# Recurrent mixer's level scores in tiles of 32 rows, and a new order of the steps in the mixers and at the seams

## The chip, the cores and the metric

The kernel runs on one core of a Trainium2 chip. The time is the device time of one execution in microseconds (us). TensorE is called PE, VectorE DVE, ScalarE ACT, GpSimd POOL and the engine that issues loads SP.

## The reference

x has 256 rows of 1024. It goes through two blocks of two layers each, all in float32. Every layer is a mixer and a gated feed-forward part (2816 wide), each added to x, with norms between:

```python
first_block:  x = x + retention_nsa_mixer(rmsnorm(x))      # stage 0
              x = x + swiglu(rmsnorm(x))                   # stage 1
              x = x + hgrn2_mixer(rmsnorm(x))              # stage 2
              x = x + swiglu(rmsnorm(x))                   # stage 3
              x = rmsnorm(x)
second_block: x = layer_norm(ALPHA * x + diff_attention(x))   # stage 4
              x = layer_norm(ALPHA * x + swiglu_2(x))         # stage 5
              x = layer_norm(ALPHA * x + chunk_attention(x))  # stage 6
              x = layer_norm(ALPHA * x + swiglu_2(x))         # stage 7
```

The recurrent mixer (stage 2) has 8 heads of 128 and computes, chunk by chunk,

```python
decay = jnp.exp(jnp.where(causal, b[:, :, :, None, :] - b[:, :, None, :, :], -jnp.inf))
attn = jnp.sum(qc[:, :, :, None, :] * decay * kc[:, :, None, :, :], axis=-1)
o = einsum(attn, vc) + einsum(qc * jnp.exp(b), state)
```

where b is the running sum of the logarithms of the forget gates. Since the decay stands inside the sum over the channels, the kernel splits the pairs (row, earlier row) by levels of 64, 32, 16, 8, 4, 2 and 1 rows: within one level the decay is a product of a factor of the row and a factor of the earlier row, and the scores of a level are matrix products.

## The kernel before

**Products.** All weights are streamed in pieces of 128x1024 numbers ("chunks", numbered through the whole program, 403 of them). SP loads a chunk into one of 4 buffers `raw`. ACT rounds it to `whi` (L2053, step HI) and POOL writes the rest `wlo = raw - whi` (L2353, step LO), each into one of 6 buffers. PE multiplies the high and low parts of the activations (`xx`, `mh`/`ml`, `hh`/`hl`) with `whi` and the high part with `wlo` (L1079, L1080, L1086). A unit is the work on one chunk for one half of the rows: four instructions with `whi` and two with `wlo`, for 128 rows and 512 columns. There are 662 units; HI of chunk c waits for the unit that used chunk c-6 last, the load of chunk c waits for LO of chunk c-4. The middle of the feed-forward stages multiplies with the weights as the stationary side (L1105, L1108).

**Side steps.** Everything else is cut into steps with two letters and a key: for instance XT (L1134) turns a quarter of x with four transposes, XH (L2099, L2102) and XL (L1471, L1475) split it into high and low parts on ACT and DVE; RES, BN, AG, RS and AP are residual, statistics and norm; SC and DC are score products (L1212, L1217) of the attentions, MK the maximum, EX the exponentials (L2201), RC and CB2 (L1659 to L1675) the combination of the two softmaxes in stage 4, TR turns the weights (L1253), AV multiplies with v. P1, P2 and P3 (L1986 to L1999, L2325) compute the scalar lambda of stage 4, RO (L1759 to L1767) is the rotation, KT turns q and k. In the recurrent mixer H1 (L1353, L1356) sums the logarithms, H2 takes exponentials on ACT, H3 (L1934 to L1938) multiplies heads and decays on DVE, H4 (`level_scores`, L1366 to L1378) is the level scores on PE, H5 (L1946, L1948) and HA collect them and O1 (L1395 to L1402) multiplies with v. A key of the mixer is (head, t), t the half of 128 rows.

**Order.** `PLAN` is a table of text, one for each of the 8 stages: "18: RC 0 0; CB2 0 0; DC 0 1 @2; TR 0 0" says that these steps stand behind unit 18 of the stage; @2 names the PSUM tile. A minus marks a step that belongs to the stage before. Every engine walks through the same table and picks its own steps, so it determines the order of instructions on each engine, between the units on PE and between the splits HI on ACT and LO on POOL. Waits are semaphores that each step counts up.

PE's tile: a product whose stationary side has 64 or 32 columns, or whose sum runs over 64 or 32 rows, uses a part of PE's array (128x64, 128x32, 64x128, 32x32); several such parts can work on different instructions. A float32 product is run in two passes, and shows as two records in the trace.

Of the kernel before, what the change touches and what calls it, by code (L numbers as in the profile page):

```python
# [17 lines left out]
FF = 2816  # L18
# [117 lines left out]
NQ, N5, N6, RQ, RK, RV, RG = 0, 512, 1024, 1304, 1816, 2328, 2840  # L136
# [172 lines left out]
62: MH 3
63: ML 3  # L310
65: RES 0 0; SQ 0 0; XT 0 0; RES 1 0
66: XH 0 0; XT 1 0; XL 0 0; XH 1 0
# [4 lines left out]
1: -SQ 0 1; -SQ 1 1; -XT 0 1; -XT 1 1; -XH 0 1  # L317
2: -RS 1; -XL 0 1
# [48 lines left out]
70: RES 0 0; SQ 0 0; B3; XT 0 0  # L367
71: XH 0 0
72: XL 0 0
74: RES 0 1; SQ 0 1; XT 0 1  # L370
# [8 lines left out]
0: -RES 1 1; -XT 1 1  # L379
1: -XH 1 1  # L380
# [2039 lines left out]
```

How the kernel before makes its waits and increments, by code:

```python
            def load(c):  # L945
                name, at, n = STREAM[c]
                if c >= NR:
                    e.wait_ge(s_lo, c - NR + 1)
                e.dma_start(raw[c % NR][:, 0:n], a[name][at:at + 128 * n].rearrange("(p m) -> p m", p=128)
                            ).then_inc(d_raw[c % NR], 16)
# [6 lines left out]
            def feed(c):  # L957
# [9 lines left out]
                    e.dma_start(w1c[:, 0, :], a["cw1k"]).then_inc(d_cw, 16)  # L967
                if c == 9:
                    e.dma_start(w2c[:, 0:64], a["cw2k"]).then_inc(d_cw, 16)
                    e.dma_start(w2c[:, 64:128], a["cw2k"]).then_inc(d_cw, 16)
                    e.dma_start(w2c[:, 128:192], a["cw2v"]).then_inc(d_cw, 16)
                if c == 10:
                    e.dma_start(w1c[:, 1, :], a["cw1v"]).then_inc(d_cw, 16)
                if c == 14:
                    e.dma_start(LC[:, 0:1024], a["ret"]).then_inc(d_ret, 16)
                if c == first[1] + 12:
                    e.wait_ge(S["R4"], 2)
                    e.dma_start(LC[:, 0:1152], a["hg"][:, 0:1152]).then_inc(d_hg, 16)
                if c == first[1] + 14:
                    e.wait_ge(s_unit, BEGIN[1])
# [2 lines left out]
                    e.dma_start(HM[:, :], a["hg"][:, 1152:1344]).then_inc(d_hn, 16)  # L983
                if c == first[3] + 12:
                    e.wait_ge(S["H5"], 16)
                    e.dma_start(GB[:, 0, :], a["fng"].partition_broadcast(128)).then_inc(d_fn, 16)
# [458 lines left out]
            def own():  # L1445
                e.wait_ge(s_dve, dv.n)
```

## Time and profile before

| | |
|---|---|
| median of three runs | 1295.08 us (1291.74 to 1297.9) |
| the profiled execution | 1292.82 us, span 1291.0 us |
| PE busy | 1275.3 us (99%) |
| POOL busy | 1030.8 us (80%) |
| ACT busy | 773.4 us (60%) |
| DVE busy | 486.0 us (38%) |
| granted TensorE clock | 0.998 |
| read from HBM | 222.59 MB, 173 GB/s |

The profile is one execution. Its timeline gives for each row the start and the length in us, the engine, the line, the operation, the tiles written and read, and in brackets how long the engine sat idle before it and what ended that. Matmuls overlap each other, so the distance between two starts says what one costs, not its length. The stages begin at these times: 0 at 0, 1 at 151, 2 at 337, 3 at 497, 4 at 684, 5 at 800, 6 at 987 and 7 at 1099 us.

### The profile page before, as it was taken

The numbers are of one execution on the slowest core, as the hardware profiler recorded it, in microseconds if no ns is written. First come the engines' busy times: TensorE is split into PE (matmuls) and PEld (weight loads), VectorE is DVE, ScalarE is ACT, GpSimd is POOL, SyncE is SP. The second block draws the span as 40 slices with busy tenths as digits, with TensorE's granted clock in tenths as the row PEclk, the third lists the DMA queues.
The fourth block names the chain that finished last, engine by engine and source line by source line (L and its number), as shares of the span: only waits on it lengthen the run. The fifth ranks groups of instructions, "written<-read, shape, count | busy, mean of one in ns | idle before, by whom it ended". The sixth has DMA issues, their size and how long they took to land.

```text
span 1291.0 us, 20471 instructions
## 1 busy us (share of the span) xinstructions
PE 1275.3 (99%) x7642; PEld 1065.2 (83%) x7642; DVE 486.0 (38%) x1080; ACT 773.4 (60%) x1481; POOL 1030.8 (80%) x874
## 2 busy tenths in 40 slices
PE   9999999999999999999999999999999999999997
PEld 7877888888888878888887787888887888888886
DVE  3465423331166752333105556232203254333302
ACT  6656576654688776666445675565534565556631
POOL 6666798878977548888889678888889987988874
PEclk9999999999999999999999999999999999999999
DMA  8443476655544425666556445666665644576552
GB/s 280 157 130 115 132 238 202 188 169 190 180 148 146 131 71 180 203 186 193 176 191 184 149 143 155 217 198 207 186 190 170 226 148 147 184 227 193 184 176 82
DMA packets 63122, 224.97 MB, mean 174 GB/s; under 512 B 7344, under 2 KB 7984, under 8 KB 63024
## 3 DMA queue, kind: packets, MB, share of 16 engines
q1 hardware_dynamic: 62736, 223.57, 55.1%
q8 instruction: 61, 1.00, 0.3%
q14 instruction: 37, 0.30, 0.1%
q10 hardware_dynamic: 288, 0.10, 0.0%
HBM read 222.59 MB, written 1.05 MB: 173 GB/s over the span
## 4 chain that ended last, share of the span: by engine, by line
PE 94%; POOL 2%; ACT 1%; DMA 1%; DVE 1%; issue 0%; SPq 0%; ACTq 0%; DVEq 0%
PE G L1079 17%; PE G L1086 17%; PE G L1080 17%; PE G L1105 10%; PE A L1105 10%; PE A L1108 5%; PE G L1108 5%; POOL wlo L2353 2%; PE A L1217 1%; PE A L1253 1%; PE A L1134 1%; DMA raw<-in_w_a 1%; PE A L1277 1%; PE A L1395 0%; PE A L1356 0%; PE A L1375 0%
## 5 line engine op out<-in xcount | busy, mean ns | idle before, releaser
L2353 POOL TENSOR_TENSOR wlo<-raw,whi 128x256 fp32r<-128x256 f32 (+2 forms) x866 | 1021.3, 1213 | 242.5 <-ACT whi L2053 242.0
L2053 ACT ACTIVATE whi<-raw 128x1024 fp32r<-128x1024 f32 x403 | 422.9, 1057 | 188.3 <-PE G L1086 162.9
L1079 PE MATMUL G<-whi,xx 128*128 128x512 f32 (+1 forms) x560 | 224.4, 401 | 3.5 <-DVE xx L1475 2.4
L1080 PE MATMUL G<-whi,xx 128*128 128x512 f32 (+1 forms) x560 | 216.8, 388 | 0.0
L1086 PE MATMUL G<-wlo,xx 128*128 128x512 f32 (+1 forms) x560 | 171.3, 388 | 0.2 <-POOL wlo L2353 0.2
L1105 PE MATMUL A<-xx,whi 128*128 128x512 f32 x576 | 144.6, 393 | 0.0
L1105 PE MATMUL G<-xx,whi 128*128 128x512 f32 x576 | 144.2, 392 | 0.0
L1079 PE MATMUL G<-whi,hh 128*128 128x512 f32 x352 | 137.4, 390 | 0.0
L1080 PE MATMUL G<-whi,hl 128*128 128x512 f32 x352 | 137.0, 389 | 0.0
L1079 PEld LDWEIGHTS G<-whi,xx 128*128 128x128 f32 x560 | 105.3, 188 | 27.8 <-issue 5.7
L1086 PEld LDWEIGHTS G<-wlo,xx 128*128 128x128 f32 x560 | 104.4, 188 | 23.0 <-POOL wlo L2353 0.6
L1080 PEld LDWEIGHTS G<-whi,xx 128*128 128x128 f32 x560 | 105.4, 188 | 18.5
L1105 PEld LDWEIGHTS A<-xx,whi 128*128 128x128 f32 x576 | 103.7, 189 | 18.7
L1105 PEld LDWEIGHTS G<-xx,whi 128*128 128x128 f32 x576 | 103.6, 189 | 18.5
L1086 PE MATMUL G<-wlo,hh 128*128 128x512 f32 x352 | 108.4, 389 | 0.0
L1108 PEld LDWEIGHTS A<-xx,wlo 128*128 128x128 f32 x576 | 78.6, 190 | 5.6
L1108 PEld LDWEIGHTS G<-xx,wlo 128*128 128x128 f32 x576 | 78.6, 190 | 5.6
L1108 PE MATMUL G<-xx,wlo 128*128 128x256 f32 x576 | 80.3, 282 | 0.0
L1108 PE MATMUL A<-xx,wlo 128*128 128x256 f32 x576 | 80.3, 282 | 0.0
L1086 PEld LDWEIGHTS G<-wlo,hh 128*128 128x128 f32 x352 | 66.1, 188 | 13.8
L1079 PEld LDWEIGHTS G<-whi,hh 128*128 128x128 f32 x352 | 66.1, 188 | 13.5
L1080 PEld LDWEIGHTS G<-whi,hl 128*128 128x128 f32 x352 | 66.1, 188 | 13.5
(385 smaller groups left out, 1504.4 us busy)
## 6 DMA issues: line engine op xcount, KB each, us to landing
raw<-in_g SPq DMA_DIRECT2D x88, 512.0 KB, 4.0
raw<-in_u SPq DMA_DIRECT2D x88, 512.0 KB, 4.2
raw<-in_d SPq DMA_DIRECT2D x88, 512.0 KB, 4.0
raw<-in_w_h SPq DMA_DIRECT2D x32, 512.0 KB, 3.6
raw<-in_w_e SPq DMA_DIRECT2D x24, 512.0 KB, 3.7
raw<-in_w_a SPq DMA_DIRECT2D x24, 512.0 KB, 3.7
raw<-in_w_b SPq DMA_DIRECT2D x24, 512.0 KB, 3.5
raw<-in_w_eo SPq DMA_DIRECT2D x8, 512.0 KB, 3.5
```

Source lines behind the costliest of these rows:

```text
L1079: e.matmul(o, sh[:, kt, xs], whi[h][:, ws], start=u.first and j == 0, stop=False)
L1080: e.matmul(o, sl[:, kt, xs], whi[h][:, ws], start=False, stop=False)
L1086: m = e.matmul(o, sh[:, kt, xs], wlo[h][:, ws], start=False, stop=u.stop and final)
L1105: e.matmul(o[:, :], whi[h][:, 128 * kt:128 * kt + 128], xx[:, kt, :], start=kt == 0, stop=False)
L1108: m = e.matmul(o[:, 0:256], wlo[h][:, 128 * kt:128 * kt + 128], xx[:, kt, 0:256], start=False, stop=kt == u.kts[-1])
L1134: m = e.transpose(A[t][:, 512 * b + 128 * i:512 * b + 128 * i + 128], X[:, t, 512 * b + 128 * i:512 * b + 128 * i + 128], ident)
L1217: m = e.matmul(tile[:, at:at + nk], qs[i], ks[i], start=not mask, stop=True, skip_group_check=True)
L1253: m = e.transpose(tile[0:kp, (i * nb + b) * 128:(i * nb + b) * 128 + 128], s[:, 2 * i if key[0] == 4 else i, 128 * b:128 * b + kp], ident)
L1277: m = e.matmul(heads4(tile[64 * g:64 * g + 64, 0:256], 2), v, wt[:, g:4:2, b, :], start=b == 0, stop=b == nb - 1, skip_group_check=True)
L2053: e.activation(whi[c % NH][:, 0:n], raw[c % NR][:, 0:n], ACT.Copy).then_inc(s_hi, 1)
L2353: m = e.tensor_tensor(wlo[c % NH][:, i:j], raw[c % NR][:, i:j], whi[c % NH][:, i:j].bitcast(F), ALU.subtract)
```

## The change

It has two parts. The first is in `level_scores`. The product of 64 rows becomes two of 32 rows, and for t = 1 the product of 128 rows becomes four of 32:

```diff
-                e.matmul(tile[0:64, 64:128], M[:, 128:192], M[:, 192:256], start=False, stop=False, skip_group_check=True)
+                for j in range(2):
+                    e.matmul(tile[32 * j:32 * j + 32, 64:128], M[:, 128 + 32 * j:160 + 32 * j], M[:, 192:256],
+                             start=False, stop=False, skip_group_check=True)
...
                 if t == 1:
-                    m = e.matmul(tile[:, 128:256], HX[:, 128 * (h % 4):128 * (h % 4) + 128], M[:, 0:128],
-                                 start=True, stop=True, skip_group_check=True)
+                    for j in range(4):
+                        c = 128 * (h % 4) + 32 * j
+                        m = e.matmul(tile[32 * j:32 * j + 32, 128:256], HX[:, c:c + 32], M[:, 0:128],
+                                     start=True, stop=True, skip_group_check=True)
```

The two diagonal products of 32x32 and the 24 small ones behind them stay as they are. That makes 40 instructions more on PE (6829 before, 6869 now).

The second part is the table `PLAN`. No step is added or removed and no unit moves; about 300 entries change their place, nearly all in stages 0, 2, 4 and 6 and at the seams. The order of POOL and SP is the same. Some lines of it (first a line of stage -1/0, then of stages 2, 4, 4, 5):

```diff
--1: -XT 0 0; -SQ 0 0; -XH 0 0; HI 0; -XL 0 0; -XT 0 1; LO 0; -XH 0 1
+-1: -XT 0 0; -SQ 0 0; -XH 0 0; -XL 0 0; HI 0; -XT 0 1; LO 0; -XT 1 0; -XH 0 1
...
-29: FJ 1; H4 0 1; H3 1 0; H1 1 1 @1
-30: H5 0 1; HA 0 1; H4 1 0; H2 1 1; GB 0 @2; HA 1 0; GC 0; EV 3 1
-31: H5 1 0; H3 1 1; T1 1 @0
-32: GF 0; H4 1 1; FB 2 @2
+28: H1 1 0 @0; H3 0 1; H2 1 1; H3 1 0; H1 1 1 @1; H4 0 1
+30: HA 0 1; H5 0 1; H4 1 0; HA 1 0; H3 1 1; GC 0; GB 0 @2; EV 3 1; H4 1 1
+31: H5 1 0; T1 1 @0
+32: GF 0; FB 2 @2
...
-2: -AP 1 1; -XT 0 1; P1; -XT 1 1; -XH 0 1
-3: P2; -XL 0 1; -XH 1 1; P3
-4: -XL 1 1; MB
-5: RO 0 0
+2: -XL 1 0; -AP 0 1; -AP 1 1; -XT 0 1; -XH 0 1
+3: -XT 1 1; -XL 0 1; -XH 1 1
+4: -XL 1 1; RO 0 0; P1; P3; MB
+6: P2
...
-18: RC 0 0; CB2 0 0; DC 0 1 @2; TR 0 0
-19: MK 0 1; EX 0 1
+18: RC 0 0; DC 0 1 @2; CB2 0 0
+19: TR 0 0; MK 0 1; EX 0 1
...
-93: AG 0; RS 0
-94: AP 0 0
-95: AP 1 0; XT 0 0; XH 0 0; XT 1 0; XL 0 0; RES 1 1
+92: RES 1 0; BN 1 0; AG 0; RS 0
+94: AP 0 0; XT 0 0; XH 0 0
+95: AP 1 0; XT 1 0; XL 0 0; RES 1 1
```

At the seam of stages 4 and 5 the entry XH 0 0 stands on ACT ahead of the split of the second feed-forward chunk instead of behind it.

The order of instructions, engine by engine, at three of these places. Line numbers of the changed kernel are lower, since its table is shorter. First PE in stage 4, before: the second tile of scores (L1212, L1217 on `G`), the turn of the first tile's weights (L1253), then a product unit.

```order
L1086 MATMUL G<-wlo,xx 128x512 x2
L1212 MATMUL G<-MB,IB 128x2x128 x2
L1217 MATMUL G<-KTa,QTa 128x256 x4
L1253 MATMUL A<-CN,W 128x128 x2
L1079 MATMUL G<-whi,xx 128x512
L1080 MATMUL G<-whi,xx 128x512
```

And in the changed kernel:

```order
L1070 MATMUL G<-wlo,xx 128x512 x2
L1196 MATMUL G<-MB,IB 128x2x128 x2
L1201 MATMUL G<-KTa,QTa 128x256 x4
L1063 MATMUL G<-whi,xx 128x512
L1064 MATMUL G<-whi,xx 128x512
L1063 MATMUL G<-whi,xx 128x512
L1064 MATMUL G<-whi,xx 128x512
L1070 MATMUL G<-wlo,xx 128x512 x2
L1237 MATMUL A<-CN,W 128x128 x2
```

The turn of the weights now stands one unit later.

Second DVE at the beginning of stage 4, before: the lambda steps (`AG`, `SM<-SM`) stand between the low parts of x (`xx<-A,xx`) and ahead of the rotation (`RT`, `PJ<-G,RT`).

```order
L1495 SCALAR_TENSOR_TENSOR X<-X,SM,LC 128x512 x2
L1986 TENSOR_TENSOR AG<-AG 128x64 x2
L1989 TENSOR_SCALAR AG<-AG 128x128
L1992 TENSOR_REDUCE SM<-AG 128x1 x2
L1475 TENSOR_TENSOR xx<-A,xx 128x4x128
L1997 TENSOR_TENSOR SM<-SM 128x1
L1999 TENSOR_SCALAR SM<-SM 128x1
L1475 TENSOR_TENSOR xx<-A,xx 128x4x128
L1624 CAST IB<-CN 128x128
L1625 CAST MB<-CN 128x128
L1759 SCALAR_TENSOR_TENSOR RT<-G,CN 128x8x32
```

And in the changed kernel:

```order
L1483 SCALAR_TENSOR_TENSOR X<-X,SM,LC 128x512 x2
L1463 TENSOR_TENSOR xx<-A,xx 128x4x128 x2
L1747 SCALAR_TENSOR_TENSOR RT<-G,CN 128x8x32
L1749 SCALAR_TENSOR_TENSOR RT<-G,CN 128x8x32
L1752 SCALAR_TENSOR_TENSOR G<-G,CN 128x512
L1755 TENSOR_TENSOR PJ<-G,RT 128x512
L1974 TENSOR_TENSOR AG<-AG 128x64 x2
L1977 TENSOR_SCALAR AG<-AG 128x128
L1980 TENSOR_REDUCE SM<-AG 128x1 x2
L1985 TENSOR_TENSOR SM<-SM 128x1
```

Both low parts of x and the first rotation now stand ahead of the lambda steps.

Third PE at the seam of stages 5 and 6, before: the last unit of stage 5 (`hh`, `hl`), two turns of a quarter of x in one row, the first unit of stage 6.

```order
L1086 MATMUL G<-wlo,hh 128x512 x2
L1134 MATMUL A<-CN,X 128x128 x8
L1079 MATMUL G<-whi,xx 128x512
L1080 MATMUL G<-whi,xx 128x512
L1079 MATMUL G<-whi,xx 128x512
```

And in the changed kernel:

```order
L1118 MATMUL A<-CN,X 128x128 x4
L1063 MATMUL G<-whi,hh 128x512
L1064 MATMUL G<-whi,hl 128x512
L1063 MATMUL G<-whi,hh 128x512
L1064 MATMUL G<-whi,hl 128x512
L1070 MATMUL G<-wlo,hh 128x512 x2
L1118 MATMUL A<-CN,X 128x128 x4
L1063 MATMUL G<-whi,xx 128x512
```

One of the two turns now stands ahead of the last unit.

## Rows read from the trace of the kernel before

**Rows 1.** The page, part 4: the chain that ended last, by engine.
```profile
PE 94%; POOL 2%; ACT 1%; DMA 1%; DVE 1%; issue 0%; SPq 0%; ACTq 0%; DVEq 0%
```

**Rows 2.** Who PE waited for: total us, times, longest.
```profile
PE G L1079 <- DVE xx L1475: 2.4, 3, 1.1
PE A L1253 <- DVE W L1675: 2.2, 1, 2.2
```

**Rows 3.** Timeline of PE, small steps in stages 2 and 4.
```profile
375.67 0.62 PE L1086 MATMUL G<-wlo,xx 128*128 128x512 f32 x2
376.22 0.33 PE L1366 MATMUL A<-W 128*64 128x64 f32 x2
376.48 0.22 PE L1368 MATMUL A<-W 128*32 128x32 f32 x2
...
376.55 0.52 PE L1375 MATMUL A<-W 128*32 128x32 f32 x36
...
377.10 0.50 PE L1079 MATMUL G<-whi,xx 128*128 128x512 f32 x1
...
382.99 0.49 PE L1378 MATMUL G<-W,HX 128*128 128x128 f32 x2
383.23 0.36 PE L1353 MATMUL A<-Wr,lf 128*128 128x256 f32 x1
...
417.23 0.42 PE L1402 MATMUL A<-PJ,DG 32*32 32x128 f32 x8
...
767.37 0.62 PE L1086 MATMUL G<-wlo,xx 128*128 128x512 f32 x2
767.82 0.60 PE L1253 MATMUL A<-CN,W 128*128 128x128 f32 x4
```

**Rows 4.** Timeline of DVE, one step of decays and the instruction behind it.
```profile
378.53 0.28 DVE L1934 TENSOR_TENSOR W<-G,QK 128x128 f32<-128x128 f32 x1
...
380.09 1.39 DVE L1886 TENSOR_TENSOR lf<-A,lf 64x512 fp32r<-64x512 f32 x2
```

**Rows 5.** Timeline of POOL at the start.
```profile
12.92 18.69 POOL L2353 TENSOR_TENSOR wlo<-raw,whi 128x1024 fp32r<-128x1024 f32 x13 [0.25 <-ACT whi L2053]
```

**Rows 6.** Timeline of all engines, beginning of stage 4.
```profile
688.35 1.03 DVE L1986 TENSOR_TENSOR AG<-AG 128x64 f32<-128x64 f32 x2 [0.34 <-DMA AG<-in_alam]
688.47 0.60 ACT L2102 ACTIVATE xx<-A 128x512 fp32r<-128x512 f32 x1 [1.50 <-PE A L1134]
...
690.26 0.68 DVE L1475 TENSOR_TENSOR xx<-A,xx 128x512 fp32r<-128x512 f32 x1
...
690.99 0.50 PE L1079 MATMUL G<-whi,xx 128*128 128x512 f32 x1 [0.74 <-DVE xx L1475]
```

**Rows 7.** Timeline of POOL, ACT and PE, first weights of stage 4.
```profile
693.82 19.54 POOL L2353 TENSOR_TENSOR wlo<-raw,whi 128x256 fp32r<-128x256 f32 x28 [0.35 <-ACT whi L2053]
...
712.52 1.06 ACT L2053 ACTIVATE whi<-raw 128x1024 fp32r<-128x1024 f32 x1 [4.27 <-DMA raw<-in_w_a]
...
717.21 0.44 PE L1253 MATMUL A<-CN,W 128*128 128x128 f32 x2 [2.20 <-DVE W L1675]
...
717.40 0.47 PE L1079 MATMUL G<-whi,xx 128*128 128x512 f32 x1
```

**Rows 8.** Timeline of PE and ACT, seam of stages 4 and 5.
```profile
797.53 0.60 PE L1134 MATMUL A<-CN,X 128*128 128x128 f32 x4
797.72 1.06 ACT L2053 ACTIVATE whi<-raw 128x1024 fp32r<-128x1024 f32 x1 [0.29 <-PE G L1086]
...
798.69 0.58 ACT L2102 ACTIVATE xx<-A 128x512 fp32r<-128x512 f32 x1
```

**Rows 9.** Timeline of DVE and PE, seam of stages 5 and 6.
```profile
982.80 0.75 DVE L1504 SCALAR_TENSOR_TENSOR X<-G,SM,LC 128x512 f32<-128x512 f32 x1 [0.33 <-ACT SM L2038]
...
985.17 1.04 PE L1134 MATMUL A<-CN,X 128*128 128x128 f32 x8
...
987.28 0.47 PE L1079 MATMUL G<-whi,xx 128*128 128x512 f32 x1 [1.07 <-DVE xx L1475]
```

More of the change, by code:

```diff
@@ L302 @@
-53: WL 2 1 1; R5 0; EV 6 1; GS 1; R1 1 @1
-54: R2V 1; R2A 1; GT 1; R6 0; R3 1; R7 0
+16: TT 0 @2
+18: TT 1 @1; CA 0 @2; CA 1 @0; CE 0; CB 0; TC 2; TT 2 @1; CD 0; EV 2 0; CB 1; CD 1; CG 0; MK 1 0 0
+19: CF 0
+20: SC 1 0 0 @1; MK 0 0 1; CE 1
+21: EX 1 0 0; EV 2 1; GE; TC 3; CF 1; EX 0 0 1; CG 1; SC 0 0 1 @2
+22: GD; NW 1 0 0
+23: TT 3 @0; NW 0 0 1; MK 1 0 1
+24: SC 1 0 1 @0
+25: RO 0 0; TR 1 0 0; CPA 1 0 0; EX 1 0 1; CPA 0 0 1
+27: AV 1 0 0; TR 0 0 1; NO 1 0 0
+28: NW 1 0 1; SC 0 0 0 @1; MK 0 0 0; AV 0 0 1; NO 0 0 1
@@ new lines @@
+43: NW 0 1 0; NW 1 1 1; WL 2 0 0; TR 0 1 0; TR 1 1 1; SC 0 1 1 @2; CPA 0 1 0; MK 0 1 1; AV 0 1 0
+44: CPA 1 1 1; NO 0 1 0; EX 0 1 1; CPV 1 1 1; SC 2 1 0 @0; AV 1 1 1; EV 5 0
+45: EX 2 1 0; NO 1 1 1; MK 2 1 0; SC 2 1 1 @1; CPA 2 1 0; EV 5 1; EX 2 1 1; WH 2 1 0
+46: NW 0 1 1; NW 2 1 0; TR 2 1 0
+47: MK 2 1 1; AV 2 1 0; NA 2 1 0; TR 0 1 1
+49: WL 2 1 0; NW 2 1 1; R1 0 @0
+50: CPA 0 1 1; GS 0; TR 2 1 1; EV 6 0; GT 0; R2V 0; CPV 2 1 1; R2A 0; CPA 2 1 1
+51: NO 0 1 1; R3 0; AV 0 1 1; AV 2 1 1
+52: NA 2 1 1; WH 2 1 1
@@ L304 @@
+53: R4 0; WL 2 1 1; EV 6 1; GS 1; R1 1 @1
+54: R5 0; R2V 1; R2A 1; R6 0; R3 1; GT 1; R7 0
 55: R4 1; R8 0
-57: R5 1; MT 2 @0; R6 1
-58: MH 2; ML 2; R7 1
-59: R8 1
+57: R5 1; MH 2; MT 2 @0; R6 1; R7 1
+59: R8 1; ML 2
 61: MT 3 @0
[L309 to L312, printed above, removed]
+62: ML 3; MH 3
+65: RES 0 0; XT 0 0; RES 1 0; SQ 0 0
+66: XH 0 0; XT 1 0; XH 1 0; XL 0 0
 68: XL 1 0
@@ L366 @@
 69: B2
[L367 to L370, printed above, removed]
+70: RES 0 0; SQ 0 0; XT 0 0; B3
+72: XH 0 0
+74: RES 0 1; XL 0 0; SQ 0 1; XT 0 1
 75: XH 0 1
 76: XL 0 1
-92: RES 1 0; SQ 1 0; XT 1 0
-93: XH 1 0
+92: RES 1 0; XT 1 0
+93: SQ 1 0; XH 1 0
 94: XL 1 0; RS 0
@@ L403 @@
-35: H2 2 0; FD 2
-36: FE 2
+18: FB 1 @1; FJ 0
+19: FA 1; EV 2 0
+20: H1 0 0 @0; T1 0 @2; FD 1; TV 0
+21: FE 1
+22: TA 0; H2 0 0; EV 2 1
+23: FG 1; H2 0 1; HA 0 0; EV 3 0
+24: H2 1 0
+25: H1 0 1 @2; FF 1; H3 0 0
+26: H4 0 0
+27: FJ 1; H5 0 0
+28: H1 1 0 @0; H3 0 1; H2 1 1; H3 1 0; H1 1 1 @1; H4 0 1
+30: HA 0 1; H5 0 1; H4 1 0; HA 1 0; H3 1 1; GC 0; GB 0 @2; EV 3 1; H4 1 1
+31: H5 1 0; T1 1 @0
+32: GF 0; FB 2 @2
+33: H5 1 1; FA 2; HA 1 1; TV 1
+35: FD 2
+36: FE 2; EV 4 0
 37: FF 2
-38: EV 4 0
-39: FG 2; EV 4 1; TA 1; GC 1; EV 5 0; H2 2 1; HA 2 0; H2 3 0
@@ new lines @@
+46: H5 2 1; H4 3 0; H2 3 1; O1 0 @0; H5 3 0; HA 3 0; H3 3 1; T1 2 @2; H4 3 1; H5 3 1
+47: O2 0; HA 3 1; O3 0; TA 2; TV 2; EV 5 1; MH 0; H2 4 0
+48: H1 4 0 @1; MT 0 @0
+49: ML 0; H3 4 0
+50: H1 4 1 @0; FB 3 @2; H2 4 1; H4 4 0
+51: H5 4 0; FA 3; HA 4 0; H3 4 1
+52: H4 4 1; H1 5 0 @1; EV 6 0; FD 3; HA 4 1; H2 5 0; FE 3
+53: H5 4 1; H3 5 0; H1 5 1 @0
+54: H4 5 0; HA 5 0; H2 5 1; FG 3; EV 6 1; FF 3; H5 5 0
+55: H3 5 1
+56: O1 1 @1; O2 1; T1 3 @2; FJ 3; HA 5 1; H4 5 1; H5 5 1; O3 1
+58: H1 6 0 @0; TA 3; TV 3; MT 1 @1
@@ L539 @@
 51: RC 3 1; CB2 3 1
[L540 to L543 removed]
+52: TR 3 1; CPA 3 1; MH 2
+53: AV 3 1; ML 2; MT 2 @0; NQ 3 1
+55: NF 3 1; MT 3 @1
 56: MH 3
@@ L704 @@
 74: RES 0 1; BN 0 1
-92: RES 1 0; BN 1 0
-93: AG 0; RS 0
-94: AP 0 0
-95: AP 1 0; RES 1 1; BN 1 1; AG 1; RS 1; AP 0 1; AP 1 1
+81: RES 1 0
+85: BN 1 0
+89: AG 0
+92: AP 0 0; AP 1 0; RES 1 1
+93: RS 0
+95: BN 1 1; AG 1; RS 1; AP 0 1; AP 1 1
 """,
```

274 lines of the change are left out of this document (108 added, 166 removed).

## The prediction

> **What bounds the kernel now.** I read the page first. PE carries 94% of the chain that ended last [rows 1], and by the table above it is busy for 1275.3 of 1291.0 us. So only two things can shorten the program: fewer or cheaper instructions on PE, or fewer of its waits. Next the table of PE's own waits [rows 2]: three waits for DVE's last step at a seam (`xx`, L1475) are 2.4 us together, one wait in stage 4 (`W`, L1675) is 2.2 us. Then the timeline of single stretches, for what one step costs and what ended each wait [rows 3 to 9].
>
> A difference of 0.5% (6.5 us) is about what a measurement of this kernel can tell from no change.
>
> The sum is made against the profiled execution, 1292.82 us (span 1291.0). The median of the three runs is 1295.08 us, 2.3 us above it; the change of the sum is applied to that median.
>
> **Level scores in 32 rows.** One step of level scores (L1366 to L1375) lasts from 376.22 to 377.10, 0.88 us, when a product follows [rows 3]. Its first instruction, 64 rows wide, goes as two passes and holds PE for 0.26 us, until the narrow ones start at 376.48. The change cuts it into two of 32 rows in different column groups, so that the whole step has one shape of tile. What two narrow pieces with 64 columns cost no row shows. Bounds: nearly nothing, if other narrow pieces cover them (0.03 us); or four passes in a row. From 376.55 on, 36 narrow passes of 32 columns take 0.52 us in four column groups, some 0.03 us a pass within one group if four run side by side, so 0.06 us for 64 columns and 0.23 us for four in a row. I take two passes in each of two groups side by side, 0.12 us, since the eight passes of 32x32 with 128 columns last 0.42 us together [rows 3], which they could not one after another at the 0.12 us of a pass of L1378 (below). That is 0.14 us less per step, 16 steps: **-2.2 us** (bounds -3.7 and -0.5).
>
> For t=1 the square product L1378 goes from 128 rows to four pieces of 32. It starts at 382.99 and the next step at 383.23, 0.24 us for two passes. Four groups side by side need the same two passes of 128 columns, 0.22 us, and PE stays in one shape of tile. I take 0.02 us less, 8 steps: **-0.2 us**. If the pieces ran in a row, eight passes of 0.11 us, it would be +0.64 us a step; that is a rival below.
>
> **Changes of the tile's shape.** From the last pair of product instructions to square transposes PE needs 0.45 us (767.37 to 767.82), to a 64-row piece 0.55 us (375.67 to 376.22) [rows 3]. So a change of the tile's shape costs some 0.09 us. Counted over PE's instructions in their order, the kernel before has 165 such changes and the changed one 138. Of the 27 fewer, 16 lie inside the level scores and are in the term above. The other 11 come from small steps now standing next to others of their shape: **-1.0 us**. The Trainium skill, TensorEngine Tiling (Array Packing), Key Properties, says that changing the tiling mode drains the engine; the 0.09 us agree with it.
>
> **The start.** PE now turns the third quarter of x before its first product. ACT can then split it sooner, and POOL, which sat idle 0.25 us at 12.92 and then ran 13 pieces without a break [rows 5], starts that chain 0.25 us earlier. PE waits for this chain once, in block 1. **-0.25 us**.
>
> **Stage 4, first wait.** On DVE the products for lambda (from 688.35) stand ahead of the step that PE's next product needs, which starts at 690.26 although ACT had written its input by then; PE waits 0.74 us until 690.99 [rows 6]. The new order puts the lambda steps behind that step and behind the first rotation. With ACT done at 689.07 the step ends before PE asks at 690.25. What is late next is nothing on PE; lambda itself is wanted only at the first combination, 25 us later. That is 0.9 us that PE gains here, 0.16 of it the engine's own restart. Moved along is one tiny exponential on ACT, behind two splits of later weights.
>
> **Stage 4, second wait.** PE has issued the second tile of scores and then waits 2.20 us for the first tile's weights, until 717.21 [rows 7]. In the new order one product unit (six instructions of 0.227 us, 1.36 us) stands between. The weights hang on ACT: it splits a piece that landed late (712.52, 4.27 us idle for the DMA) ahead of the exponentials. That load was issued when POOL had finished seven pieces in a row from 693.82 on, with 0.35 us idle ahead of them. So the weights come at most 0.35 us sooner, 716.86, however early PE is. Before, the second product unit after the scores starts at 717.40 + 1.36 = 718.76. Now it starts at 716.86 + 0.19 (the two transposes) = 717.05. Both waits together: **-1.7 us**, not the 3.3 us that the two seem worth, and PE still waits 1.3 us there.
>
> **Seam of stages 4 and 5.** The turned x is ready at 797.53 + 0.60 = 798.13, but ACT starts the split of a weight at 797.72 and reaches it at 798.69; PE then waits for the last of the three waits of [rows 2], 2.4 - 0.74 - 1.07 = 0.6 us [rows 8]. In the new order the split stands behind. That is 0.56 us sooner: **-0.55 us**. The weight split is used some twelve units later.
>
> **Seam of stages 5 and 6.** DVE has normed the first quarter at 982.80 + 0.75 = 983.55, yet PE turns it at 985.17, behind the last product unit, and waits 1.07 us until 987.28 [rows 9]. Now the turn stands one unit earlier, so ACT and DVE work under that unit. The wait goes, 1.2 us with the restart. Late next is the third quarter: DVE norms it only behind the residual and the statistics of the last one, and with PE 1.2 us ahead I expect 0.2 us before its turn and 0.2 us before the product after. **-0.8 us** (bounds -1.2 and 0).
>
> **Waits that the new order adds.** About thirty other PE steps are moved by one to three units, and in the trace most have 0.2 to 1.4 us between their last input and their start, which is less than a unit. Their inputs on DVE and ACT are moved too. No row shows what is left over. Bounds: 0, and 4 us (a quarter of a unit at a dozen places). I take **+0.6 us**, nearer to nothing, since where I followed the order by hand (the first heads of the recurrent mixer, the second pair of stage 6) the inputs came in time.
>
> Sum: -2.2 -0.2 -1.0 -0.25 -1.7 -0.55 -0.8 +0.6 = **-6.1 us**. That gives 1286.7 us for the profiled execution and **1289.0 us** for the median, 0.47% less: at the edge, but within 0.5%.
>
> **Rivals.**
> 1. *All of it comes.* No new waits, narrow pieces fully covered, the weights of stage 4 a unit's worth sooner. Then -3.7 in place of -2.2, nothing for +0.6, and 1.3 us more in stage 4: 9.5 us less, 1285.6 us. For it: PE waits nowhere else, so nothing is there to absorb a gain. Against it: POOL's unbroken run holds the load of 712.52 [rows 7].
> 2. *The narrow pieces run one after another.* Then L1366's successor gains 0.03 us and the square product loses 0.64 us: -0.5 + 5.1 in place of -2.4, 1296.0 us. The Trainium skill, TensorEngine Tiling, Instruction Overhead, gives each matmul a fixed cost of some 60 cycles. By an estimate from that page at 2.4 GHz the 40 added instructions (80 passes) would take back 2 us of this term. Against both: 36 narrow passes fit in 0.52 us [rows 3].
> 3. *Slower: the recurrent mixer waits for DVE.* The new order lets level scores of two halves follow each other directly in some places (both halves of the second head, for one). Before each, DVE has a step of decays, 378.53 to 380.09, 1.56 us [rows 4]. If PE stood for one such step ahead of nine of the 16 level scores, that is +14.0 us on -6.1: 1303.0 us. It decides from four such waits on (6.1 us), and from nine it is beyond 0.5%. Against it: DVE's inputs are moved forward too, and PE is never idle in this mixer before.
> 4. *The order gives and takes alike.* New waits at the upper bound, 4 us, and nothing from the seam of stages 5 and 6: 1293.2 us.
>
> **How the numbers follow.** The forecast, 0.62; I split it at the edge, 0.27 over and 0.35 under 0.5%, since its own spread is about 2 us and runs of before spread by 3 us either way. Rival 1: 0.15. Rival 2: 0.06. Rival 3: 0.06. Rival 4: 0.11. So faster 0.27 + 0.15 = 0.42, same 0.35 + 0.06 + 0.11 = 0.52, slower 0.06. The range goes from 1284 (rival 1 with half a run's spread) to 1294.5 (rival 4 with some); rival 3 and most of rival 2 lie outside.
>
> **What would show it.** Right: a level-score step of 0.74 us where a product follows; PE's table of waits without the three for `xx`, with the wait for `W` in stage 4 down to about 1.3 us; the turn of x ahead of the last unit of stage 5. Wrong: the successor of L1366 taking 0.23 us before the next narrow pieces begin; PE waits for DVE of over 3 us in stages 0 and 2; or a row "PE waits for POOL" that grew, since POOL is then late with a split that it now has ready in time.

## The result and the profile after

The changed kernel takes 1284.31 us (median of six runs, 1284.19 to 1284.54), the kernel before 1293.73 in the same comparison (1291.07 to 1298.89): ratio 0.9923, 95% interval 0.9907 to 0.9938. That is 9.4 us or 0.7% less, beyond the forecast of 1289.0. (That stood on the first median, 1295.08; from 1293.73 the same sum would give 1287.6.) The profiled execution went from 1292.82 to 1284.46 us, 8.4 us less. Two things stand out at once: more was gained than the sum of 6.1 us, and the runs, which spread over 8 us before, now lie within 0.4.

The page of the kernel after, parts 1 and 4 [rows 1]:

```profile
PE 1271.4 (99%) x7722; PEld 1062.0 (83%) x7722; DVE 483.7 (38%) x1080; ACT 766.2 (60%) x1481; POOL 1029.6 (80%) x874
...
PE 97%; POOL 1%; ACT 1%; DMA 0%; DVE 0%; issue 0%; ACTq 0%; DVEq 0%; POOLq 0%
```

PE has 97% of the chain in place of 94%. Who PE waited for, kernel after: these three rows are all there are [rows 2].

```profile
PE A L1099 <- DVE spread L1515: 1.2, 1, 1.2
PE A L1118 <- DMA X<-in_x: 1.1, 1, 1.1
PE G L1104 <- DVE PJ L1429: 1.1, 1, 1.1
```

The three waits for `xx` (L1475) are gone, and the wait for `W` in stage 4 is gone too, of which I had left 1.3 us standing. The rows for `spread` and `PJ` stand in the kernel before as well, with the same lengths. The wait for `X` does not: at the start PE now turns the third quarter ahead of its first product, and waits for its load. In its place the profile of before has a wait of 0.9 us for the first `xx` (L1471).

The first product unit of each stage shows where the time went. The spans between them, kernel after less kernel before, in the two profiled executions:

```
stage        0      1      2      3      4      5      6      7
us       -0.73   0.00  -3.42  +0.07  -3.16  -1.35  +0.31  -0.07
```

**Level scores** [rows 3]. Timeline of PE, one step with t=0 and what follows it:

```profile
375.51 0.25 PE L1351 MATMUL A<-W 128*32 128x64 f32 x2
375.53 0.25 PE L1354 MATMUL A<-W 128*32 128x32 f32 x2
375.59 0.23 PE L1351 MATMUL A<-W 128*32 128x64 f32 x2
...
375.70 0.51 PE L1361 MATMUL A<-W 128*32 128x32 f32 x35
...
376.24 0.50 PE L1063 MATMUL G<-whi,xx 128*128 128x512 f32 x1
```

The step takes 0.73 us in place of 0.88 (I had forecast 0.74). The pieces of the next pair (L1354) begin 0.02 us behind the first of L1351, and those of L1361 from 375.65 on: the four pieces overlap across column groups. Over all 16 steps, from each record's start to the next one's, the step's lines take 13.19 us in place of 16.47.

**Stage 4** [rows 7]. Timeline of ACT, DVE and PE of the kernel after, around its first weights:

```profile
706.13 1.06 ACT L2041 ACTIVATE whi<-raw 128x1024 fp32r<-128x1024 f32 x1 [2.94 <-DMA raw<-in_w_a]
...
710.15 0.61 DVE L1663 SCALAR_TENSOR_TENSOR W<-A,SM,W 128x128 f32<-128x128 f32 x2
...
711.39 0.38 PE L1237 MATMUL A<-CN,W 128*128 128x128 f32 x2
```

PE turns the weights at 711.39 without a wait; they were written at 710.15 + 0.61 = 710.76. ACT still waits for the load, 2.94 us in place of 4.27. The load itself took 5.5 us from issue to landing and 7.4 before. My sum had held the landing fixed. The issue itself came about as said, 21.0 us behind the stage's first product in place of 21.4. The experiments start from there.

**The seams** [rows 8, 9]. ACT at the seam of stages 4 and 5: the turned x is taken ahead of the weight pieces now.

```profile
791.42 0.60 ACT L2090 ACTIVATE xx<-A 128x512 fp32r<-128x512 f32 x1 [0.73 <-PE A L1118]
791.92 2.00 ACT L2041 ACTIVATE whi<-raw 128x1024 fp32r<-128x1024 f32 x2
```

PE at the seam of stages 5 and 6: the turn stands ahead of the last unit (L1063 with `hh`), and the next stage's first unit follows without a wait.

```profile
976.50 0.60 PE L1118 MATMUL A<-CN,X 128*128 128x128 f32 x4
976.86 0.48 PE L1063 MATMUL G<-whi,hh 128*128 128x512 f32 x1
...
978.34 0.60 PE L1118 MATMUL A<-CN,X 128*128 128x128 f32 x4
978.69 0.47 PE L1063 MATMUL G<-whi,xx 128*128 128x512 f32 x1
```

### The profile page after: what moved, and what is told of

Same layout as the page of the kernel before. It is cut to its first block, busy times and chain, and to the rows that moved or that the text cites. A ratio compares the mean times of both kernels' runs of the same rounds, so it can differ in the third digit from the quotient of the medians.

```text
span 1282.7 us, 20629 instructions
## 1 busy us (share of the span) xinstructions
PE 1271.4 (99%) x7722; PEld 1062.0 (83%) x7722; DVE 483.7 (38%) x1080; ACT 766.2 (60%) x1481; POOL 1029.6 (80%) x874
## 4 chain that ended last, share of the span: by engine, by line
PE 97%; POOL 1%; ACT 1%; DMA 0%; DVE 0%; issue 0%; ACTq 0%; DVEq 0%; POOLq 0%
PE G L1063 18%; PE G L1070 18%; PE G L1064 18%; PE G L1089 10%; PE A L1089 10%; PE A L1092 5%; PE G L1092 5%; POOL wlo L2341 1%; PE A L1201 1%; PE A L1118 1%; PE A L1237 1%; PE A L1261 1%; PE A L1340 0%; PE G L1201 0%; PE A L1361 0%; DMA CP<-in_cols 0%
## 5 line engine op out<-in xcount | busy, mean ns | idle before, releaser
L1063 PE MATMUL G<-whi,xx 128*128 128x512 f32 (+1 forms) x560 | 226.4, 405 | 0.4
L1063 PE MATMUL G<-whi,hh 128*128 128x512 f32 x352 | 137.5, 391 | 0.0
L1063 PEld LDWEIGHTS G<-whi,xx 128*128 128x128 f32 x560 | 105.2, 188 | 26.3 <-issue 6.2
L1063 PEld LDWEIGHTS G<-whi,hh 128*128 128x128 f32 x352 | 66.1, 188 | 13.5
```

The source lines that it names most:

```text
L1063: e.matmul(o, sh[:, kt, xs], whi[h][:, ws], start=u.first and j == 0, stop=False)
```

## Experiments

All medians stand beside runs of the kernel before on the same chip, at 1293.5 to 1294.7 us. I quote the ratio to those with its interval, and sizes of single places from the profiles. The e kernels ran on one chip, the f kernels on a second, the g kernels on a third and the h kernels on a fourth, so medians of different letters, and of the kernel after, are not from one chip; where I subtract them, the profile's figure stands beside. Each kernel has one profile.

**The two parts of the change apart.** e1 is the kernel before with these lines of the change (and the same for the square product):

```diff
-                e.matmul(tile[0:64, 64:128], M[:, 128:192], M[:, 192:256], ...)
+                for j in range(2):
+                    e.matmul(tile[32 * j:32 * j + 32, 64:128], M[:, 128 + 32 * j:160 + 32 * j], M[:, 192:256], ...)
```

> The kernel before with only the level scores in pieces of 32 rows; the order of all steps is that of before. Theory A (the prediction's terms): 16 steps save 2.4 us, of it 0.12 us per step with a product behind it: 1291.4 us if before is at 1293.7. Theory B (from the trace after): the step is cheaper than I had it. With t=0 it goes from 0.86 us to 0.65, with t=1 from 1.10 to 0.85, and its entry is cheaper too; the time from a step's start to the next one's, summed over the 16, fell from 16.16 to 11.61 us: 4.5 us less, 1289.2 us. Theory C: what PE gains in these steps it gives back by waits, since DVE and ACT are then late: the steps are short in the trace, but the time falls by 1 us or less. Spread of the runs: before spread over 8 us and after over 0.4; if that spread comes from the loads of stage 4, it stays wide here.

Measured: 1289.51 us, ratio 0.9966 (0.9954 to 0.9978), so 4.0 us less. But the trace does not put this into the level scores. They went from 16.47 to 13.55 us, -2.9 us, between A and B. Another 1.6 us came from stage 4, where not a line differs: PE's wait for `W` is not there. (That place gained 2.3 us; PE's wait for `xx` at the stage's begin grew from 0.7 to 1.4 us, which gave 0.7 back.) C is out. The profile is the lowest of e1's five runs, and they spread over 2.7 us, so the wait may still be there in others.

e2 is the changed kernel with the old `level_scores`.

> The changed kernel with the level scores of before, 64 rows for the first piece and 128 for the square product: the new order alone. Theory A (the prediction's terms): -1.0 for eleven changes of shape (only seven of them are left with the old level scores), -0.25, -1.7, -0.55, -0.8, +0.6 = -3.7 us. Theory B (the trace after less the level scores, -8.3 + 4.5): -3.8 us in the profile, of it some 3.2 in stage 4 and its seam. The two agree in the sum and differ in the places: A has stage 4 with its seam at -2.2, B at -3.2 and recurrent mixer at +1. Spread of the runs: narrow as after's, if it is the order of stage 4 that took the wait for the loads away.

Measured: 1288.84 us, ratio 0.9958 (0.9946 to 0.9970), 4.6 us less. By places the profile has -0.94 us in stage 0, -0.25 in stage 2 (no loss of 1 us, so B fails there), -3.22 in stage 4, and -0.82 in stages 5 and 6 together (-1.34 and +0.52). No wait for `W` here either. The two medians add up to the whole within 1 us, but not because the parts are independent: each of them alone removes the same wait, so in the profiles they sum to 9.8 us and the whole is 8.4. e3 and e4 take the new order of one stage alone.

> The kernel before with the new order in stage 4 alone (its begin, its heads, and the begin of the seam behind it); old level scores, old order in all other stages. Theory A (the prediction's terms): both waits of stage 4 -1.7 and the seam behind it -0.55, so -2.25 us, and PE still waits 1.3 us for the first weights. Theory B: the trace after shows no wait for these weights at all, since the load that ACT waited for took 5.5 us from issue to landing instead of 7.4: -3.2 us against the profiled execution, more (4 to 5) against a median of before in which that load is often slow. Under B the runs of this kernel spread over less than 1 us, as after's do, and those of before over several; under A the spread stays, since the wait stays. Rival: the spread comes from another place, then it stays as well, but the profile has no wait for W.

Measured: 1291.50 us, ratio 0.9981 (0.9972 to 0.9989), spread 1289.6 to 1292.2. That is theory A's size, and PE's wait for `W` stands in the profile with 1.6 us. So B's forecast for this order failed: the order alone does not remove the wait.

> The kernel before with the new order in stage 2 alone (recurrent mixer), old level scores. The order removes one change of the tile's shape there while the old pieces stand. Theory A (the prediction's terms): nearly nothing, -0.1 to +0.3 us. Theory B: stage 2 gained 3.4 us in the trace after, while its level scores alone gained 4.5, so the new order itself costs some 1.1 us here: +1.1. Rival to B: the order only fits the shorter level scores, and with the old ones it gains or loses something else, beyond 1.5 us either way.

Measured: 1292.69 us, ratio 0.9991 (0.9980 to 1.0001); stage 2 itself gained 0.24 us. The order there alone is worth nearly nothing: theory A.

So the same order of stage 4 goes with 2.2, 1.4 or no wait for `W` (before, e4, e1), and something outside the stage decides. The load that ACT waits for is issued behind the layer norm's rows. The next four experiments take those rows away and move the two pieces of the stage singly. The first of them, f1:

```diff
-                if c == first[4] + 12:
+                if c == first[4] + 20:
                     e.wait_ge(S["AP"], 4)
                     gb_rows(0)
```

> The kernel before, with one number changed on the load queue: the two loads of the layer norm's rows (lng and lnb, 512 KB each) are issued eight weight pieces later, some 22 us, in stage 4. In the six profiles so far the weight load behind them took 4.8 to 7.7 us to land (other weight loads 3.6), and ACT's wait for it, 1.5 to 5.2 us, went with it. Theory A (these rows make the wait for the weights W in stage 4, and the spread of the runs with it): the load lands in 3.6 us, ACT waits under 1 us, PE's wait for W is gone, the runs spread over less than 1 us, and the median falls by 2 to 3 us to about 1291. Theory B (the load is late for another reason, POOL's seven pieces in a row): ACT still waits 3 to 4 us, PE 1 to 2 us for W, the median stays within 0.7 us and the spread too. A loss is possible if the rows now come late for the layer norm at the stage's end: then PE waits longer for xx there.

Measured: 1290.57 us, ratio 0.9979 (0.9969 to 0.9988). Eleven of twelve runs lie between 1290.4 and 1291.1, and PE's table has no wait for `W` in stage 4. Theory A holds: the rows' loads ahead of it make this load late, and that costs the kernel before 2.7 us by the ratio, 3.4 by the medians; in the profile stage 4 is 2.3 us shorter. (The twelfth run is the profiled one, 1295.64; it lost 5.0 us in stage 0, see the last section.)

> The changed kernel with the same late rows. In its profile PE has no wait for W, and its six runs spread over 0.4 us. Theory A: its order has room for the late load, so this gives nothing: within 0.5 us of 1284.3. Theory B (its runs only happened to have quick loads, and its median moves when the loads are slow): a gain of 0.5 to 2 us and the lowest time of all.

Measured: 1284.51 us, spread 0.5, ratio 0.9929 (0.9916 to 0.9941). Theory A: nothing to gain in the changed kernel. It does not suffer from the rows.

> The kernel before with only DVE's lambda products, ACT's tiny exponential and the copy of the mask moved behind the first rotation at the begin of stage 4. Theory A (the first wait of stage 4, as predicted): PE's wait of 0.74 us for xx at the begin of stage 4 is gone, -0.9 us at the first unit after it. But if the wait for W stands behind it and hangs on a load (the chain that ends last there is POOL and the load queue), the gain is taken back 25 us later: the median falls by under 0.3 us. Theory B (the loads follow PE closely enough): the whole 0.9 us is seen in the median.

Measured: 1294.29 us, ratio 1.0000 (0.9990 to 1.0009). The first wait is gone from PE's table (1.7 us in two waits for `xx`, 2.4 in three before), yet nothing is gained: the later wait for `W` grew to 3.5 us. Theory A.

> The kernel before with only the turn of the first weights of stage 4 (TR 4 0 0) one product unit later on PE. Theory A: PE's wait for W shrinks by the unit that now stands before it, 1.36 us, or is gone where it was shorter; the median falls by 1.2 to 1.4 us, and the spread of the runs shrinks by as much at its lower end only. Theory B: something hangs on the turn (the copy of the weights, the product with the values, the free bank) and takes it back: under 0.5 us.

Measured: 1292.03 us, ratio 0.9985 (0.9977 to 0.9994), 1290.4 to 1293.9; the wait for `W` is down to 1.2 us. That is 1.9 us less, theory A and somewhat more than its 1.4 us.

The profile of f3 is the longest of its twelve runs and shows what such a run contains. Granted clock of PE in stretches of f3 (core, us, PE busy and count, PEclk, DMA share, GB/s):

```profile
708.00:713.00 5.00, 5.00 (x26) 1.00 0.96 341
713.80:717.30 3.50, 0.00 (x0) 0.86 0.50 160
717.30:722.90 5.60, 5.59 (x14) 0.50 0.32 94
722.90:727.00 4.10, 4.10 (x19) 0.97 0.00 0
```

PE was idle from 713.8 to 717.3, and then the granted clock is 0.50, the lower of its two levels (1.2 GHz), until 722.9. Passes of 512 columns start 0.43 us apart instead of 0.23:

```profile
717.31 0.69 PE L1253 MATMUL A<-CN,W 128*128 128x128 f32 x2 [3.52 <-DVE W L1675]
717.65 0.78 PE L1079 MATMUL G<-whi,xx 128*128 128x512 f32 x1
718.23 0.63 PE L1080 MATMUL G<-whi,xx 128*128 128x512 f32 x1
718.65 0.63 PE L1079 MATMUL G<-whi,xx 128*128 128x512 f32 x1
```

Eleven such steps at 0.20 us more and a slower start at 717.31 are some 2.6 us. Stage 4 lost 3.0 us against the kernel before (+1.3 in the wait, -0.9 at the stage's begin, +2.6 in clock). In the profiled execution of before the granted clock stays at 1.00 behind its wait of 2.2 us.

The longer runs of the kernel before were not profiled, but each run has its mean granted clock, and the time goes with it. Of 77 runs beside these experiments, 14 have 0.999 (mean 1292.3 us), 28 have 0.998 (1293.3), 30 have 0.997 (1294.7) and 5 have 0.996 (1296.4). No run of f1, f2, g1, g2 or the kernel after is below 0.998. One stretch like that of f3, 5.6 us at half the clock, is 0.2% of the mean. So the upper half of the spread fits the wait for `W` with a fall of the clock behind it; that is an inference from the mean, not seen in a trace of before.

**What makes the load late.** Three kernels put the old order of stage 4 back into the changed kernel (g1), join the new order of that stage with the late rows (g2), and take the square product alone (g3).

> The changed kernel with the old order put back in stage 4 and its seam alone. Theory A (what takes the late load out of PE's way is the order of stage 4): the wait for W is back with 1 to 4 us in the profile, the runs spread over 3 us or more, and the median rises by 2.5 to 5 us over 1284.3. Theory B (the load comes quicker in the changed kernel, since all before it stands otherwise): the spread stays under 1 us and only the two short waits come back: +0.9 at the begin of stage 4 and +0.5 at the seam, 1285.8.

Measured: 1286.16 us, ratio 0.9936 (0.9924 to 0.9949), spread 1.3. Theory B: only 1.85 us of the change's gain hang on the order of stage 4 (1.5 in the profiles: 1.6 at the begin and 0.5 at the seam, less 0.6 between). The load is quick in the changed kernel, whatever the order.

> The kernel before with the new order of stage 4 and also the layer norm's rows loaded eight pieces later: the stage's order without the load's luck. The rows alone gave 1290.5 us. Theory A: the first wait (-0.9) and the seam (-0.55) come on top of that: 1289.1 us, with a spread under 0.7 us. The second wait has nothing left to give, since the weights are there in time. Theory B (the load still decides when PE may go on): no more than 0.5 us below 1290.5.

Measured: 1289.66 us, ratio 0.9962 (0.9948 to 0.9975), 0.9 us below f1 and not 1.45. Against f1's profile stage 4 has -0.97 at the begin and -0.51 at the seam, and +0.5 in between. Small steps and product units take turns more often in the new order (27 stretches of product in the stage in place of 19), which fits that loss but was not tested by itself.

> The kernel before with only the square product of the level scores (t=1, 8 steps) in four pieces of 32 rows; the first piece stays at 64 rows. Theory A (the pieces run side by side in four column groups): 0.02 to 0.05 us less a step, -0.2 to -0.4 us in stage 2. Theory B (they run one after another): +0.64 us a step, +5.1 us. With A nearly all of the gain of the level scores hangs on the first piece: the two steps of a pair go from 0.31 us to 0.11.

Measured: 1290.26 us, ratio 0.9966 (0.9954 to 0.9978). Stage 2 gained 0.23 us, as theory A has it, for all eight steps. Yet the median fell by 4.4 us, and stage 4 is 2.2 us shorter in the profile. An edit worth 0.23 us removed the wait for `W`.

The traces of all these runs have one thing in common. The page of queues lists fetches of instructions, 16 KB each, on queue 8. For each kernel: when the fetch nearest to the rows' issue starts, when the load queue issues the rows' first load and how long that issue takes, the time from that issue to landing, and PE's wait for `W`:

```
kernel    fetch    issue    took   landing  wait for W   times
before    702.45   702.65   1.09    6.1      2.2         1291.0 to 1298.9
e3        702.46   702.56   1.20    6.6      1.6         1289.6 to 1292.2
e4        701.53   702.03   0.82    5.6      1.4         1290.8 to 1294.8
f3        701.75   702.06   1.02    6.9      3.5         1291.3 to 1295.6
f4        702.24   702.64   0.93    6.2      1.2         1290.4 to 1293.9
e2        700.38   701.05   0.63    4.4      none        1287.5 to 1289.7
e1        708.32   700.36   0.43    4.4      none        1288.3 to 1291.0
g1        707.43   699.18   0.43    4.6      none        1286.0 to 1287.3
g3        693.03   702.06   0.43    4.5      none        1290.0 to 1291.1
after     705.02   698.14   0.43    4.4      none        1284.2 to 1284.5
```

In the five kernels with the wait a fetch starts 0.1 to 0.5 us ahead of the issue; e2 lies at the edge, with 0.67 us and an issue lengthened by 0.2 us. g3 has 24 PE products more ahead of this place than before, and e1, g1 and the kernel after have 40; their fetches stand elsewhere. Queue 8 of the kernel before between 702.4 and 702.6 (packets, MB, share of 16 engines), and the four issues of such rows in the program, of which only the one at 702.65 takes 1.09 us:

```profile
q8 instruction: 1, 0.02, 29.0%
```

```profile
L953 SPq DMA_DIRECT2D LC<-in_lng x4: 431/432/1089, 702.7 to 1126.9; - x4
```

So far this is a coincidence seen ten times. Three kernels test it both ways, with PE instructions that do nothing:

```diff
                 o = G[u.bank][:, 512 * u.t:512 * u.t + n]
+                for _ in range(4 if u.st == 2 and i < BEGIN[2] + 24 else 0):
+                    e.wait_ge(s_hi, 1)
```

(four such waits become two instructions; h2 has 42 and h3 46 in place of 24, on the changed kernel).

> The kernel before with 48 more instructions on PE that do nothing: semaphore waits that are long satisfied, two ahead of each of the first 24 product units of stage 2. They move the fetches of PE's instructions against its work by some 5 us. Theory A (the fetch of 16 KB that starts 0.2 us before the rows' issue makes the load late): the fetch now comes 4 to 6 us ahead of the rows' issue, this issue takes 0.43 us, PE's wait for W is gone, the median falls by 2.5 to 3.5 us to about 1290.7 although the kernel does more, and the runs spread over 1.5 us or less. Theory B (the fetch has nothing to do with it; the level scores and the order moved something else): the median stays within 0.7 us of before's, or rises with the waits' own cost, and the spread of 5 us stays.

Measured: 1290.96 us, ratio 0.9980 (0.9971 to 0.9989), 1290.6 to 1293.1, so 2.6 us less by the ratio and 3.6 by the medians, for a kernel that does more than before. The fetch came at 696.73, 5.8 us ahead; load queue of this kernel:

```profile
702.52 0.43 SPq L953 DMA_DIRECT2D LC<-in_lng  x1
702.99 0.43 SPq L954 DMA_DIRECT2D LC<-in_lnb  x1
```

PE's wait for `W` is 0.4 us, and stage 4 is 1.8 us shorter in the profile. Theory A; the spread of 2.5 us is wider than it had.

> The changed kernel with 84 such waits (42 units of stage 2), which should move a fetch of PE's instructions to just ahead of the rows' issue: between the two there are now 82 PE records in the trace. Theory A: if the fetch starts 0 to 0.7 us before the issue, the issue takes 0.6 us or more, the weight load behind it 6 us or more, ACT's wait for it grows from 2.9 to 4 to 5 us; PE waits for W by 0 to 2 us, and the runs spread over 1 us or more. Theory B: nothing but the waits' own cost, the same spread of 0.4 us. The place of the fetch varies by some instructions, so it may miss; then this run says nothing, and the trace shows by how much.

> As the run with 84 waits, with 92 (46 units of stage 2): the fetch some 0.7 us sooner. One of the two should meet the rows' issue. Theory A and B as there.

Measured: h2 1286.23 us (1286.05 to 1287.94), ratio 0.9944 (0.9929 to 0.9958); h3 1285.74 us (1284.29 to 1286.20), ratio 0.9935 (0.9918 to 0.9952). Both met the issue, the fetch at 697.75 and 697.64. Load queue of h2, then PE's wait for `W` in h2 and in h3:

```profile
697.86 1.26 SPq L937 DMA_DIRECT2D LC<-in_lng  x1
699.16 0.43 SPq L938 DMA_DIRECT2D LC<-in_lnb  x1
```

```profile
PE A L1239 <- DVE W L1665: 1.9, 1, 1.9
```

```profile
PE A L1239 <- DVE W L1665: 0.9, 1, 0.9
```

Theory A again: the wait that the changed kernel had lost is back, with the spread (1.9 us in both) and 1.4 to 1.9 us in the median, of four runs each. In the profiles stage 4 is 3.6 us (h2) and 1.2 us (h3) longer than in the kernel after, and stages 0, 2, 5 and 6 are as there within 0.25 us, so the waits themselves cost nothing. In h2's profile PE's granted clock is 0.72 between 715 and 720. That the fetch beside the issue makes the loads late is shown. Why the issue then takes longer, and the transfers behind it, no trace here says.

The profiles hold one more such meeting that nobody arranged. In g3 a fetch starts at 1002.01, 0.45 us ahead of the rows' issue of stage 6. That issue takes 0.85 us and its load lands after 5.6; in the other 17 profiles the same issue takes 0.43 us and the load 4.2 to 4.9.

```profile
1002.46 0.85 SPq L953 DMA_DIRECT2D LC<-in_lng  x1
```

The weights' own issues do not suffer. In all profiles, from 40 us on, 300 of them have a fetch that starts between 0.7 us before and 0.2 us after. All 300 take 0.33 us, and their loads land after 3.7 us in the median, those of the others after 3.9.

**A version faster than both.** If a change of tile shape costs what the sum said, the output step of the recurrent mixer has some to give: it alternates seven times between products of 128 rows and pieces of 32. g4 writes all six large products first and the sixteen pieces behind them.

```diff
                         if t == 1:
                             e.matmul(tile[:, x:x + 128], HX[:, 128 * (h % 4):128 * (h % 4) + 128], v0, ...)
+                for t in range(2):
+                    for i in range(2):
+                        h, x = 2 * u + i, 256 * t + 128 * i
+                        v = PJ1[:, t, ub + 512 + 128 * i:ub + 640 + 128 * i]
                         for j in range(4):
```

> The changed kernel with the recurrent mixer's output step (four of them) regrouped: first the six products with tiles of 128 rows of both heads and both row blocks, then the sixteen of 32 rows. Same instructions, same sums; 24 changes of the tile's shape fewer (138 to 114). Theory A (a change costs 0.09 us): -2.2 us, 1282.1 us, and the step falls from 3.44 to 2.9 us in the trace. Theory B (the price lies in the pieces' entry and overlap, not in the change): under 0.7 us. A loss of some tenths is possible, if the values' weights can't be loaded ahead across the group.

Measured: 1281.66 us, ratio 0.9901 (0.9887 to 0.9914). The four steps went from 13.75 to 10.98 us, 0.115 us for each of the 24 changes. The price may hold more than the change of shape, since pieces side by side also overlap over a longer stretch. g4 leaves part of the sums out: it starts the accumulation on four regions of the bank one after another, and pieces added later to the first regions overwrite what stands there. h4 marks the start on the bank's first product alone (`start=x == 0`).

> The regrouped output step of the recurrent mixer on the changed kernel once more, now with the start of accumulation marked on the first product of the bank alone, since the first try's marks on the later ones threw the earlier sums away. Same instructions, so the same time: 1281.7 us within 0.3, 2.6 us below the changed kernel; by the trace of the first try the four steps give all of it.

Measured: 1281.45 us (1281.43 to 1281.74), ratio 0.9904 (0.9891 to 0.9918), 2.9 us below the changed kernel (3.0 by the profiles). One output step on the timeline of PE in h4:

```profile
414.58 0.91 PE L1383 MATMUL A<-PJ,MX 128*128 128x128 f32 x6
415.32 0.39 PE L1386 MATMUL A<-PJ,HX 128*128 128x128 f32 x2
415.54 0.39 PE L1383 MATMUL A<-PJ,MX 128*128 128x128 f32 x2
415.77 0.39 PE L1386 MATMUL A<-PJ,HX 128*128 128x128 f32 x2
416.08 1.07 PE L1394 MATMUL A<-PJ,DG 32*32 32x128 f32 x32
```

In the kernel after, the same step has its pieces in four groups (L1390 at 415.20, 415.96, 416.96 and 417.95). PE is now early enough to wait for DVE once at a level score, the first sign of rival 3 (and once more in stage 2, 0.5 us at L1324):

```profile
PE A L1351 <- DVE A L1930: 0.6, 1, 0.6
```

## Why the prediction was right or wrong

The forecast was 1289.0 and it came to 1284.3; within 0.5% was the likeliest case, and the change is 0.7%. The lower end of the range, 1284, was reached, but by a path that no term or rival described. Without the late load the rest of the sum came out near: f1 (kernel before, load in time) 1290.6 less kernel after 1284.3 is 6.3 us, where the terms other than the second wait of stage 4 had 5.3, or 5.9 without the new waits that did not come. By its steps:

- *Stage 4, second wait* is the step that failed. Both waits of the stage together were to give 1.7 us; by the 22nd unit of the stage the profile has 3.2. The prediction said: "So the weights come at most 0.35 us sooner, 716.86, however early PE is", and left 1.3 us of waiting. That took the landing of one load, 7.4 us in one execution, for a property of the kernel. It came in 5.5 us. The change had moved a fetch of PE's instructions away from the issue of the rows ahead of it, and such a meeting alone brings the late load or takes it away (h1 to h3). I had read that ACT waited for the DMA, and never asked why this load took twice as long as its neighbours (3.6 us).
- *The median* hid a second part of the same error. I set the sum of one execution, whose wait was 2.2 us, against a median of runs in which the wait, and by the mean clocks the clock behind it, cost more: f1 shows 2.7 to 3.4 us. A spread of 6 us over three runs was on the first page I read and was taken for noise.
- *Level scores*: -2.4 forecast, -2.9 in e1 and -3.3 in the kernel after. Right in kind, the step cheaper by 0.03 us than taken in e1; the rest comes with the new order. One reading in it was wrong: 36 passes in four groups within 0.52 us are 0.058 us a pass, not 0.03. The figure taken, 0.12 us for the first pieces, is two passes by the right one, so it held by luck. The square product was -0.23 in all (g3), forecast -0.2. Rival 2 is out: 0.23 us less where it had +5.1.
- *Changes of shape*: 0.09 us forecast, 0.11 in g4 and h4. The term of -1.0 spreads over stages 0, 2 and 6 and can't be read apart; stage 0 as a whole gained 0.7 to 0.95 us where this term and the start gave 0.6 (kernels with the old order there differ by 0.5 us among themselves, f1 left out). The Trainium skill, TensorEngine Tiling (Array Packing), Key Properties, says a change of tiling mode drains the engine. A price of 0.11 us at each change agrees with that; that it is a drain no trace shows.
- *Stage 4, first wait* -0.9, measured -0.97 (g2). *Seam of stages 4 and 5* -0.55, measured -0.5. But the first gives nothing while the wait for the load stands behind it (f3), and half a microsecond was lost between the two places (g2), which no term had.
- *Seam of stages 5 and 6* -0.8, measured -1.35 and +0.31 behind it, -1.0 together. The third quarter is late as said: PE goes on at 981.81, 0.28 us after its unit was through.
- *New waits* +0.6, measured none: the table of PE's waits has no row for DVE that the kernel before has not. Rivals 3 and 4 did not come.
- Rival 1 (1285.6 us) is nearest, but for a reason that it did not name: it let the weights come "a unit's worth sooner" without saying what would make the load quicker.

## What to carry to other kernels

When runs of a kernel spread by more than the gain you look for, find the wait that varies before you price anything: compare one load's time to landing with its neighbours', and look what else the queues carried at its issue. A small edit of one engine's instruction count can move such a meeting, so check an edit's gain in the trace at the place of the edit (by the profiles g3 had four fifths of its gain and e1 a third in a stage that neither touched). And group matrix products by the shape of their tiles, within a step too: 0.11 us each time is 2.7 us for a reordering of the same products, if the start of accumulation is marked anew (h4).

## What the runs showed of the hardware that I had not expected

- A fetch of 16 KB of instructions that starts 0.1 to 0.5 us before the issue of a load of rows lengthens that issue from 0.43 to 0.8 to 1.3 us and the landing from 4.4 to between 5.6 and 6.9 us, and the weight load behind it lands late too (after 6.6 to 8.1 us in the seven profiles with such a meeting at this place, 4.7 to 5.6 in the eight others that have the rows there). Loads of weights issued beside a fetch are not lengthened (300 of 300).
- A wait of 3.5 us on PE was followed by 5.6 us at the lower clock, a loss of 2.6 us (f3). Behind the 1.9 us of h2 the clock fell too, for 3.4 us, and behind the 3.3 us of f1 (next point) for as long; behind the 2.2 us of before it did not. So a wait's price can be over its length, and its length alone does not tell.
- One DVE instruction of 128x4 elements took 4.36 us once, in the profiled run of f1, where its like take 0.2; PE waited 3.3 us for it and then had the granted clock 0.50 until 93.3, which is the rest of the 5.0 us that stage 0 lost. It is seen in one profile of all, and its cause is open:

```profile
84.91 0.17 DVE L1698 RECIPROCAL SM<-SM 128x4 f32<-128x4 f32 x1
85.11 4.36 DVE L1700 TENSOR_TENSOR SM<-SM 128x4 f32<-128x4 f32 x1
89.50 0.69 DVE L1708 TENSOR_TENSOR W<-G,SM 128x512 f32<-128x512 f32 x1
```

PE behind it (us, busy and count, PEclk, DMA share, GB/s):

```profile
87.00:90.20 3.20, 0.00 (x0) 0.95 0.54 164
90.20:93.30 3.10, 3.05 (x14) 0.50 0.59 169
93.30:97.00 3.70, 3.70 (x26) 1.00 0.00 0
```

- A start of accumulation on one region of a bank also ends the sums of its other regions, for what is added to them later (g4 and h4). The Trainium skill, Advanced Engine Details and Errata, PSUM Accumulation, says that the first product of a group clears the written marks of the bank, in the groups of 32 partitions that it writes; g4's products write all 128, and the two kernels agree with it.
